# Order of TensorE's work in a step of prompt attention: transposes ahead of scores

## The reference

```python
def window_prompt(q, kv):
    ...
    s = jnp.einsum('bnqkgd,bnskd->bnkgqs', qb, band[:, :, :, 0]).astype(jnp.float32) * ATTN_SCALE
    ...
    p = jax.nn.softmax(jnp.where(m, s, NEG_INF), axis=-1).astype(q.dtype)
    o = jnp.einsum('bnkgqs,bnskd->bnqkgd', p, band[:, :, :, 1])
```

## Time and profile before

| | us |
|---|---|
| median of 3 runs | 2266.71 |
| lowest and highest run | 2264.95, 2268.06 |
| span of the profiled execution | 2267.7 |
| TensorE matmuls busy over the span | 1961.3 (86%) |
| VectorE busy | 938.9 (41%) |
| ScalarE busy | 718.4 (32%) |

### The profile page before, as it was taken

One profiled execution on the slowest core, in us unless ns is written; L12 is line 12 of the kernel. 1 busy time (PEld: TensorE's weight loads), 2 busy tenths in 40 slices (PEclk: granted clock), 3 DMA queues, 4 the chain that ended last, 5 costly groups with the idle time before them and its releaser, 6 DMA issues. The chain is left out here.

```text
span 2267.7 us, 31652 instructions
## 1 busy us (share of the span) xinstructions
PE 1961.3 (86%) x11453; PEld 1691.5 (75%) x11453; DVE 938.9 (41%) x1711; ACT 718.4 (32%) x1165; POOL 32.9 (1%) x49
## 2 busy tenths in 40 slices
PE   4689887969979898997677498699999999999995
PEld 2289765537866676775355397699999999999994
DVE  1332556014455555563332622644434444344334
ACT  1321151004435354442111401555323333333222
POOL 1000000000100000000000000000000000000000
PEclk8889998988879898988788799799999999999997
DMA  8012254033500000002140111344445444545341
GB/s 296 16 42 46 74 167 155 0 135 112 181 17 1 1 0 1 1 0 116 84 187 3 28 47 37 88 134 129 121 139 148 130 130 122 156 129 145 111 114 77
DMA packets 296079, 205.24 MB, mean 91 GB/s; under 512 B 20125, under 2 KB 283853, under 8 KB 292750
## 3 DMA queue, kind: packets, MB, share of 16 engines
q1 hardware_dynamic: 290174, 166.61, 25.6%
q0 software_dynamic: 4016, 37.84, 4.3%
q10 hardware_dynamic: 1824, 0.02, 0.0%
HBM read 197.15 MB, written 11.41 MB: 92 GB/s over the span
## 5 line engine op out<-in xcount | busy, mean ns | idle before, releaser
L477 PE MATMUL banks<-ff_h_hi,ff_hi 128*128 128x352 f32 x1056 | 341.9, 324 | 26.8 <-DVE ff_h_lo L473 26.8
L479 PE MATMUL banks<-ff_h_hi,ff_lo 128*128 128x352 f32 x1056 | 341.4, 323 | 0.0
L478 PE MATMUL banks<-ff_h_lo,ff_hi 128*128 128x352 f32 x1056 | 339.8, 322 | 0.0
L473 DVE TENSOR_TENSOR ff_lo<-ff_raw,ff_hi 128x2048 fp32r<-128x2048 f32 (+1 forms) x114 | 229.3, 2012 | 190.8 <-ACT ff_hi L469 190.8
L469 ACT ACTIVATE ff_hi<-ff_raw 128x2048 fp32r<-128x2048 f32 (+1 forms) x114 | 192.2, 1686 | 184.1 <-PE banks L479 181.1
L477 PEld LDWEIGHTS banks<-ff_h_hi,ff_hi 128*128 128x128 f32 x1056 | 198.7, 188 | 27.4 <-issue 27.4
L478 PEld LDWEIGHTS banks<-ff_h_lo,ff_hi 128*128 128x128 f32 x1056 | 200.5, 190 | 0.0
L479 PEld LDWEIGHTS banks<-ff_h_hi,ff_lo 128*128 128x128 f32 x1056 | 198.6, 188 | 0.0
L477 PE MATMUL banks<-hid_hi,ff_hi 128*128 128x352 f32 x528 | 172.6, 327 | 6.1 <-DVE hid_lo L473 6.1
L479 PE MATMUL banks<-hid_hi,ff_lo 128*128 128x352 f32 x528 | 172.2, 326 | 0.0
L478 PE MATMUL banks<-hid_lo,ff_hi 128*128 128x352 f32 x528 | 171.6, 325 | 0.0
(11 more groups left out here) (328 smaller groups left out, 3191.7 us busy)
## 6 DMA issues: line engine op xcount, KB each, us to landing
ff_raw<-in_w_gate SPq DMA_DIRECT2D x66, 512.0 KB, 4.0
ff_raw<-in_w_up SPq DMA_DIRECT2D x66, 512.0 KB, 5.3
ff_raw<-in_w_down SPq DMA_DIRECT2D x48, 384.0 KB, 4.1
late_ada<-in_w_ada SPq DMA_DIRECT2D x32, 512.0 KB, 4.8
ff_raw<-in_w_down SPq DMA_DIRECT2D x48, 320.0 KB, 3.4
s_raw<-in_w_in SPq DMA_DIRECT2D x48, 128.0 KB, 2.3
x_nat<-in_x_prompt SPq DMA_DIRECT2D x2, 2048.0 KB, 22.2
hT<-in_w_ada SPq DMA_DIRECT2D x2, 2048.0 KB, 42.1
```

Source lines behind the costliest of these rows:

```text
L473: return dve.tensor_tensor(lo, raw, hi.bitcast(F32), ALU.subtract)
L477: pe.matmul(out, lhsT=w_hi, rhs=x_hi, start=first, stop=False)
L478: pe.matmul(out, lhsT=w_hi, rhs=x_lo, start=False, stop=False)
L479: return pe.matmul(out, lhsT=w_lo, rhs=x_hi, start=False, stop=last)
```

## The change

In TensorE's part of the steps the transposes of unit u-2 are issued ahead of the scores of unit u. The sum of unit u-3 stays last. The waits inside `turn`, `qk` and `pv` are the same. The queues of the other engines stay as they are.

```diff
@@ -1568,10 +1568,10 @@
                 for u in range(2, U + 3):
+                    if u < U + 2:
+                        turn(u - 2)
                     if u < U:
                         qk(u)
-                    if u < U + 2:
-                        turn(u - 2)
                     if u >= 3:
                         pv(u - 3)
```

## The result

The changed kernel takes 2277.94 us (median of eight executions, 2271.49 to 2324.33), the kernel before 2267.39 in the same comparison (2264.49 to 2325.74). The ratio is 1.0045, with a 95% interval of 1.0028 to 1.0061: slower by 0.45%, where 2277.0 us and +0.45% were forecast. One of these eight executions and two of the kernel before took some 2.5% longer, which is where the ranges end; the ratios leave them out.

What follows compares the result with a forecast made beforehand. TensorE's own work was taken as the bound. Terms of 6.9 (bank-5 waits), 2.2 (start chain) and 1.2 us (seams) summed to 10.3 us, taking the median from 2266.71 to 2277.0 us, +0.45%; range 2271 to 2285.

Steps and rivals of the forecast that it cites:

- (b): Transposes ask for bank 5 sooner and TensorE waits for VectorE's copy, queued behind its maximum: 1.73 us an iteration, 6.9 in all.
- (c): At an iteration's start, transposes lengthen the chain from probabilities through scores and exponential: about 0.55 us an iteration, 2.2 in all.
- (a): Three seams between kinds of matmul on TensorE change: about 0.01 us a step longer, 1.2 us in all, bounds -8.1 to +11.6.
- Bank 4 is no such case: Claim that transposes into bank 4 meet no wait like bank 5's, as ScalarE copies it ahead of its exponential.
- The open seam: A sum's first weight load behind a mask product, shown by no row; taken to hide, otherwise up to +0.10 us a step.
- Seams pay: Rival: transposes behind a sum and scores behind transposes save 0.07 us a step; 2267.7 us; chance 0.10 together with missing waits.
- The waits don't come: Rival: TensorE is already late by other work, only (a) and (c) stay; 2270.1 us; chance 0.10 shared with seams paying.
- a bank free in time with seams that pay: Rival: seams save time and TensorE does not wait for bank 5; 2258.6 us; chance 0.03.
- A dear seam: Rival: the sum's first load comes a whole 0.11 us pitch behind the mask product, +11.6 us; 2287.4 us; chance 0.07.
- The clock falls: Rival: holes in an iteration's last steps drop the clock to 1.2 GHz, some 3.2 us an iteration; 2290 us; chance 0.03.

Runs made afterwards that it cites:

- the fourth experiment: Changed kernel with transposes first only where the transposed unit has over four key tiles, and VectorE's copy ahead of its maximum: 2269.61 us, ratio 1.0001 to the kernel before.

## Why the prediction was right

The sum was 10.3 us, or 2.58 an iteration. Measured are 9.0 in the stage as profiled, 9.3 with filled starts, and 10.6 between the medians. That the median came out within 1 us of the forecast is partly luck: the change itself is 1 us smaller than the sum, and the terms' errors partly cancel. By its terms, per iteration, from the first iteration's steps:

| term | predicted | measured, from |
|---|---|---|
| (b) copy behind the maximum | 1.73 | 1.55 (80.33 - 78.78), 1.54 (79.70 - 78.16) |
| (c) start chain with (a), seams | 0.55 and 0.3 | 0.75 (78.78 - 78.03, all seams), 0.79 (78.82 - 78.03, seams of small units) |
| (a) seams of large units | a share of 0.3 | 0.13 (78.16 - 78.03), 0.19 of it holes |

(b) was right in cause, place and size. By starts of weight loads the six waits are 0.04, 0.08, 0.22, 0.35, 0.48 and 0.62 us, 1.79 in sum; predicted were 0.02, 0.08, 0.21, 0.34, 0.47 and 0.61. They cost 1.55, about 0.04 less each. Part of the reason is a row that I hadn't thought of: behind a held transpose the scores' load starts at the same moment (1055.04), where without a hold it comes 0.11 later (754.29, 754.40), and about half of that is still there one load on.

(c) was right that the chain lengthens and too small in holes. I let it close with a hole at two closings for t = 0 and one for t = 1. In the changed kernel the last iteration has six, of 0.67, 0.46, 0.06, 0.24, 0.14 and 0.06 us by starts of loads, 1.6 in sum, where before it had some 0.5. These 1.1 us cost less than their length, 0.75 with the seams in the first iteration, where the holes at the start sum to 1.2 (0.1 before). The step that failed is the sentence "Bank 4 is no such case: ScalarE copies it ahead of its exponential". In one step that is so, but the copy that the transposes of u wait for is that of u-1, and it stands right behind the exponential of u. Before the change TensorE's next instruction, the scores, needed the exponential only. Its second record ends at 981.67, and the load of the scores comes 0.06 later, at 981.73:

```profile
981.48 0.19 ACT L1592 ACTIVATION_READ_ACCUMULATOR hT<-banks,neg_max 128x1 f32 x1
```

Now the transposes close the chain, 0.28 behind that record and 0.11 behind the end of ScalarE's copy, at 986.60 as at 988.87. With the longer copy of two tiles, at 991.35, it is 0.39 and 0.11, and so it is in all four iterations. The copy makes 0.22 us of each of the first two holes and the whole third, together some 0.7 of the 1.1 us. Without it the second hole would be 0.12 longer than before the change, where 0.13 was predicted. This is read from the trace; no run moved this copy.

(a) was right within its accuracy. The open seam, mask product to sum, hides wholly, as I took it: the sum's first load is at 1048.76, the same as the mask product's. The rest answers the sum of loads: ten of the sum 1.07 us (1052.90 to 1053.97), then eight transposes up to the scores 0.89 (1050.28 to 1051.17), together 1.96; before it was 0.83 + 1.12 = 1.95 (from the earlier trace rows). The range of -8.1 to +11.6 us was needlessly wide: had I laid the two sequences of loads side by side like this, the only unknown left was one load. The Trainium skill's rule on which weight loads overlap a running matmul (TensorE: Matmul & The Clock Gate, Part 3, The mechanism) comes to nil for the seams, and this agrees in its result; the hidden loads themselves, that of the sum at 1048.76 among them, are of full height and overlap all the same. The same section also lets a load into the background weight buffer go ahead of running matmuls; whether that is what happens here no trace shows.

The rivals. *Seams pay*: excluded by the 0.13 us of the fourth experiment. *The waits don't come*: excluded by the line of waits. (Its neighbour, a bank free in time with seams that pay, was put at 2258.6 without the 2.2 us of (c); 2260.8 is meant.) *A dear seam*: excluded by 1048.76. *The clock falls*: did not happen in the changed kernel, and the reason I gave against it, that holes of this size don't lower the clock in the earlier trace rows, was too simple. I looked for it at the end of the iteration, where the holes are 0.6 us in 7; it does threaten at the start, in near relatives of this kernel, and costs 36 to 60 us an iteration, not the 3.2 that I put on it. My 3% was for a mild form of it; the severe form was not among the rivals.

What stays open is why the clock rises and stays up in one iteration and not in another. Shown are two ways in which it stays low (it doesn't rise behind L1568, or rises and falls in the early steps), the price, and that the moment at which it fell or rose ahead of the steps separates the iterations of each kind. A cause is not shown.

## What to carry to other kernels

When a TensorE order asks for a bank sooner, follow the bank's release through the queue of the engine that frees it: what stands ahead of the freeing instruction there (here the maximum of scores that only just ended) sets the wait, and its sum by shapes came out within 0.1 us an iteration (1.73 predicted, 1.79 waited). Do this for every bank that the moved instruction asks for, and for the neighbouring unit's copy, not only the one of the same step: bank 4's was dismissed too early. Lay the sequences of weight loads of both orders side by side before giving seams a price. And when a reordering opens holes where the clock has just risen, take many executions and read the granted clock of each stretch: one iteration of the same matmuls at half the clock costs some 60 us, the change 9, and filling the start of a loop with wide matmuls of no use gained 0.37% here.

## What was not expected of the hardware

- An iteration of 570 matmuls lasts 92.70 us at a granted clock of 0.91 and 153.00 at 0.50, and TensorE, busy in all 112.00 of 112.00 us, stayed at 1.2 GHz. Neither a busy TensorE nor the wide matmuls of L1568 always bring 2.4 GHz back.
- With waits of 0.62 us and less taken out (copy ahead of the maximum) the kernel took 4.2% longer than the changed one (2373.26 against 2277.94 us), though its steps with the clock up are 1.55 us shorter. In its profiled execution (2424.0 us) three of four iterations ran mostly at 1.2 GHz.
- With the clock falling 16.87 us ahead of the steps it was back at 2.4 GHz at their start, with 16.97 us it stayed at 1.2 GHz for the whole iteration, TensorE's work being the same.
- VectorE's gap of 2.81 us between iterations took in an added instruction of 0.82 us and moved the next start by 0.14 us.
